# Turning the inverse of the delta rule over: VectorE in 32x32 blocks at levels 0 to 4, TensorE at level 5

## The reference

```python
k_beta = k * beta[..., None]
lower = jnp.where(strict, jnp.einsum('bhncd,bhnsd->bhncs', k_beta, k) * decay, 0.0)
rhs = jnp.concatenate([v * beta[..., None], k_beta * jnp.exp(g)[..., None]], axis=-1)
sol = lax.linalg.triangular_solve(lower, rhs, left_side=True, lower=True, unit_diagonal=True)
u, w = jnp.split(sol, 2, axis=-1)
```

## Time and profile before

| what | value |
|---|---|
| median of 3 runs | 4044.71 us (4038.54 to 4046.26) |
| the profiled execution | 4045.38 us, span 4043.6 us |
| mean granted TensorE clock | 0.976 |
| PE busy | 3901.0 us, 96% of the span |
| PEld busy | 3107.4 us, 77% |
| DVE busy | 2286.6 us, 57% |
| ACT busy | 1542.9 us, 38% |
| POOL busy | 491.4 us, 12% |

### The profile page before, as it was taken

The page is one execution under the profiler, slowest core; times in us unless marked ns, Lnnn a source line. Parts: engine busy times, 40 slices in busy tenths (PEclk is TensorE's granted clock), DMA queues, the critical chain, the costliest instruction groups (busy, mean ns, idle before and its releaser), DMA issues. The chain is left out here.

```text
span 4043.6 us, 47189 instructions
## 1 busy us (share of the span) xinstructions
PE 3901.0 (96%) x18086; PEld 3107.4 (77%) x18086; DVE 2286.6 (57%) x3149; ACT 1542.9 (38%) x2242; POOL 491.4 (12%) x366
## 2 busy tenths in 40 slices
PE   8999989999999998999989999999999999999997
PEld 6888668888788865888867678788877667878886
DVE  5445765445544565645567643675576663376656
ACT  3224643223322464322343534343343443443333
POOL 1001720000000163100020012200010002220002
PEclk9999989999999998999999989999999999999999
DMA  4333103333233320333331100122233100023222
GB/s 149 98 98 111 58 21 99 95 99 108 89 98 95 109 68 16 98 98 98 108 104 63 42 6 1 53 94 99 94 106 103 54 32 1 6 74 99 94 99 78
DMA packets 87022, 315.05 MB, mean 78 GB/s; under 512 B 10016, under 2 KB 10400, under 8 KB 86176
## 3 DMA queue, kind: packets, MB, share of 16 engines
q1 hardware_dynamic: 83664, 302.43, 23.5%
q10 hardware_dynamic: 3152, 9.74, 0.7%
HBM read 307.94 MB, written 2.10 MB: 77 GB/s over the span
## 5 line engine op out<-in xcount | busy, mean ns | idle before, releaser
L381 ACT ACTIVATE wh<-raw 128x1024 fp32r<-128x1024 f32 x564 | 597.4, 1059 | 1631.0 <-PE ps L401 1317.4
L399 PE MATMUL ps<-xh,wh 128*128 128x512 f32 x2336 | 918.0, 393 | 16.0 <-DVE xl L464 9.3
L400 PE MATMUL ps<-xl,wh 128*128 128x512 f32 x2336 | 910.8, 390 | 0.0
L401 PE MATMUL ps<-xh,wl 128*128 128x512 f32 x2336 | 910.7, 390 | 0.0
L385 DVE TENSOR_TENSOR wl<-raw,wh 128x1024 fp32r<-128x1024 f32 x564 | 694.2, 1231 | 190.9 <-ACT wh L381 190.1
L399 PEld LDWEIGHTS ps<-xh,wh 128*128 128x128 f32 x2336 | 439.8, 188 | 112.6 <-issue 19.8
L400 PEld LDWEIGHTS ps<-xl,wh 128*128 128x128 f32 x2336 | 439.9, 188 | 94.3 <-issue 3.6
L401 PEld LDWEIGHTS ps<-xh,wl 128*128 128x128 f32 x2336 | 439.7, 188 | 91.3
L399 PE MATMUL ps<-fh,wh 128*128 128x512 f32 x1016 | 397.4, 391 | 4.0 <-DVE wl L385 4.0
L400 PE MATMUL ps<-fl,wh 128*128 128x512 f32 x1016 | 395.4, 389 | 0.0
L401 PE MATMUL ps<-fh,wl 128*128 128x512 f32 x1016 | 395.4, 389 | 0.0
(11 more groups left out here) (465 smaller groups left out, 5656.6 us busy)
## 6 DMA issues: line engine op xcount, KB each, us to landing
raw<-in_w SPq DMA_DIRECT2D x564, 512.0 KB, 3.5
con<-in_consts SPq DMA_DIRECT2D x1, 2052.5 KB, 13.9
h<-in_x SPq DMA_DIRECT2D x4, 512.0 KB, 7.0
p_t<-in_p ACTq DMA_DIRECT2D x4, 512.0 KB, 4.3
w1k<-in_w1c ACTq DMA_DIRECT2D x2, 1024.0 KB, 4.9
w1v<-in_w1c ACTq DMA_DIRECT2D x2, 1024.0 KB, 7.2
out<-h SPq DMA_DIRECT2D x8, 256.0 KB, 2.1
dup_k<-roped ACTq DMA_DIRECT2D x8, 128.0 KB, 3.5
```

What stands on the lines that cost most here:

```text
L381: nc.scalar.activation(wh[k % 2][:, :], raw[k % 4][:, :], ACT.Copy).then_inc(s["w_hi"], 1)
L399: nc.tensor.matmul(DB[k % 2][:, :], a, hi(q), start=(q == order[0]), stop=False)
L400: nc.tensor.matmul(DB[k % 2][:, :], a, lo(q), start=False, stop=False)
L401: last = nc.tensor.matmul(DB[k % 2][:, :], b, hi(q), start=False, stop=(q == order[-1]))
```

## The change

At levels 1 to 4 the inverse is non-zero only within diagonal blocks of at most 32 tokens, so a transpose of each 32x32 block on its place is a transpose of the whole. Level 0 to 4 are now turned over by one VectorE instruction for each head, from `tri_t` straight to `tri` (both in SBUF), in the new function `dve_turn`. TensorE's transposes and ScalarE's copies of those levels are gone; level 5 keeps them, with a semaphore of its own (`tri_turned`). At levels 1 to 4 `dve_turn` stands right behind the subtraction of its head, inside `dve_upper`'s loop, and so ahead of the second head's subtraction and of all that follows in VectorE's queue. For level 0 of a later pair it stands ahead of the subtractions of level 6. In the first pair, the 14 idle matmuls keep their place in TensorE's queue. Pieces 10 and 11 of `pe_pre` are gone, and so are `act_tri0` and its place in ScalarE's queue.

```diff
--- before.py
+++ after.py
@@ -1568,7 +1568,8 @@
                     dve.wait_ge(s["tok_exp"], 1)
                     v.tensor_tensor(beg, bet, eg, ALU.mult).then_inc(s["kb_ready"], 1)
 
-                PIECES, READS = 12, 9
+                PIECES, READS = 10, 9
+                BLOCKS32 = 4
                 OFF = [0, 512, 896, 1152, 1280]
                 HEADS = (3, 4, 6, 7, 0, 1, 5, 2)
                 HSUM = {0: 0, 1: 2, 3: 4, 4: 6, 5: 8, 6: 10, 7: 12, 2: 14}
@@ -1599,9 +1600,12 @@
                 def pre_reader(t, i):
                     if i < READS:
                         return "pre_read", READS * t + i + 1
-                    if i == READS:
-                        return "eg_ready", t + 1
-                    return "tri_ready", PIECES * t + i - READS
+                    return "eg_ready", t + 1
+
+                def tri_count(t, lv, hd):
+                    if lv > BLOCKS32:
+                        return "tri_turned", 2 * t + hd + 1
+                    return "tri_ready", 2 * ((BLOCKS32 + 1) * t + lv) + hd + 1
 
                 def pe_pre(pe, s, t, i):
                     mm, tr = nc.tensor.matmul, nc.tensor.transpose
@@ -1626,13 +1630,8 @@
                     elif i < 9:
                         for b in range(NB):
                             ins = tr(bank[:, blk_of(b)], qkv[:, (3 if i == 7 else 6) + t, blk_of(b)], c("ident"))
-                    elif i == 9:
+                    else:
                         ins = mm(bank[:, :], c("pick2")[0:6, t * P:(t + 1) * P], g6, start=True, stop=True)
-                    else:
-                        hd = i - 10
-                        pe.wait_ge(s["tri0"], 2 * t + hd + 1)
-                        for b in range(NB):
-                            ins = tr(bank[:, blk_of(b)], tri_t[t % 2][hd][:, b, :], c("ident"))
                     ins.then_inc(s["pre_mm"], 1)
 
                 def dve_pre(dve, s, st, t, i):
@@ -1673,6 +1672,17 @@
                                                 c("ident").unsqueeze(1).to_broadcast([P, NB, P]), dec[hd][:, :, :],
                                                 ALU.subtract).then_inc(s["tri0"], 1)
 
+                def dve_turn(dve, s, t, lv, hd):
+                    if lv:
+                        dve.wait_ge(s["inv_ready"], turn(t, lv, hd) + 1)
+                    else:
+                        dve.wait_ge(s["tri0"], 2 * t + hd + 1)
+                        if t:
+                            dve.wait_ge(s["u_mm"], turn(t - 1, LEVELS, hd) + 1)
+                    nc.vector.transpose(tri[hd][:, :, :].rearrange("p b f -> p (b f)"),
+                                        tri_t[t % 2][hd][:, :, :].rearrange("p b f -> p (b f)"))\
+                        .then_inc(s["tri_ready"], 1)
+
                 def dve_qg(dve, s, st, t):
                     dve.wait_ge(s["eg_ready"], t + 1)
                     nc.vector.tensor_tensor(qkv[:, t, :], e_g[:, :], qkv[:, t, :], ALU.mult).then_inc(s["qg_ready"], 1)
@@ -1685,19 +1695,14 @@
                     act.wait_ge(s["pre_mm"], PIECES * t + 10)
                     nc.scalar.activation(e_g[:, :], pre_bank(t, 9)[:, :], ACT.Exp).then_inc(s["eg_ready"], 1)
 
-                def act_tri0(act, s, st, t):
-                    for hd in range(2):
-                        act.wait_ge(s["pre_mm"], PIECES * t + 11 + hd)
-                        nc.scalar.activation(tri[hd][:, :, :], view(pre_bank(t, 10 + hd)), ACT.Copy)\
-                            .then_inc(s["tri_ready"], 1)
-
                 def turn(t, lv, hd):
                     return (t * LEVELS + lv - 1) * 2 + hd
 
                 def pe_lower(pe, s, t, lv):
                     for hd in range(2):
                         pe.wait_ge(s["b_ready"], turn(t, lv, hd) + 1)
-                        pe.wait_ge(s["tri_ready"], PIECES * t + 2 * (lv - 1) + hd + 1)
+                        name, value = tri_count(t, lv - 1, hd)
+                        pe.wait_ge(s[name], value)
                         for b in range(NB):
                             ins = nc.tensor.matmul(DB[hd][:, blk_of(b)], low[hd][:, b, :], tri[hd][:, b, :], start=True,
                                                    stop=True)
@@ -1728,8 +1733,8 @@
 
                 def act_turned(act, s, st, t, lv):
                     for hd in range(2):
-                        act.wait_ge(s["tt_mm"], (t * (LEVELS - 1) + lv - 1) * 2 + hd + 1)
-                        nc.scalar.activation(tri[hd][:, :, :], view(DB[hd]), ACT.Copy).then_inc(s["tri_ready"], 1)
+                        act.wait_ge(s["tt_mm"], 2 * t + hd + 1)
+                        nc.scalar.activation(tri[hd][:, :, :], view(DB[hd]), ACT.Copy).then_inc(s["tri_turned"], 1)
 
                 def dve_upper(dve, s, st, t, lv):
                     for hd in range(2):
@@ -1737,6 +1742,8 @@
                         x = tri_t[t % 2][hd]
                         nc.vector.tensor_tensor(x[:, :, :], x[:, :, :], view(DB[hd]), ALU.subtract)\
                             .then_inc(s["inv_ready"], 1)
+                        if lv <= BLOCKS32:
+                            dve_turn(dve, s, t, lv, hd)
 
                 def pool_mask(pool, s, st, src, dst, level, name):
                     nc.gpsimd.tensor_tensor(dst[:, :, :], src[:, :, :],
@@ -2284,9 +2291,8 @@
                         pe_pre(pe, s, 0, i)
                     pe_sb(pe, s, 0)
                     for i in range(3, PIECES):
-                        if i == 10:
-                            pe_idle(DB[0], 0, 14)
                         pe_pre(pe, s, 0, i)
+                    pe_idle(DB[0], 0, 14)
                     pe_sb(pe, s, 1)
                     for t in range(GT):
                         for lv in range(1, LEVELS + 1):
@@ -2295,8 +2301,6 @@
                             pe_lower(pe, s, t, lv)
                             if slot < 15:
                                 pe_sb(pe, s, slot + 2)
-                            if lv == 6 and more:
-                                pe_pre(pe, s, t + 1, 10)
                             pe_upper(pe, s, t, lv)
                             if t and lv == 1:
                                 pe_out(pe, s, t - 1, 0)
@@ -2304,7 +2308,7 @@
                                 pe_new(pe, s, t - 1, lv - 1)
                             if more and lv <= 5:
                                 pe_pre(pe, s, t + 1, 2 * lv - 2)
-                            if lv < LEVELS:
+                            if BLOCKS32 < lv < LEVELS:
                                 pe_turned(pe, s, t, lv)
                             if t and 2 <= lv <= 4:
                                 pe_out(pe, s, t - 1, lv - 1)
@@ -2314,7 +2318,7 @@
                                 else:
                                     pe.wait_ge(s["eg_ready"], 1)
                                 pe_idle(BK[2], 0, 8)
-                            if more:
+                            if more and lv <= 5:
                                 pe_pre(pe, s, t + 1, 2 * lv - 1)
                         if not more:
                             pe_idle(BK[0], 0, 4)
@@ -2345,7 +2349,6 @@
                     act_sb(act, s, st, 0)
                     act_eg(act, s, st, 0)
                     act_sb_late(act, s, st, 0)
-                    act_tri0(act, s, st, 0)
                     act_sb(act, s, st, 1)
                     for t in range(GT):
                         for lv in range(1, LEVELS + 1):
@@ -2356,10 +2359,8 @@
                                 act_sb(act, s, st, slot + 2)
                             if lv == 2 and more:
                                 act_dec(act, s, st, t + 1, 0)
-                            if lv < LEVELS:
+                            if BLOCKS32 < lv < LEVELS:
                                 act_turned(act, s, st, t, lv)
-                            elif more:
-                                act_tri0(act, s, st, t + 1)
                             if lv == 2 and more:
                                 act_dec(act, s, st, t + 1, 1)
                             if lv == 5 and more:
@@ -2397,6 +2398,8 @@
                         dve_pre(dve, s, st, 0, i)
                     dve_qg(dve, s, st, 0)
                     dve_tri0(dve, s, st, 0)
+                    dve_turn(dve, s, 0, 0, 0)
+                    dve_turn(dve, s, 0, 0, 1)
                     dve_sb_late(dve, s, st, 1)
                     red = None
                     for t in range(GT):
@@ -2405,6 +2408,9 @@
                             more = t + 1 < GT
                             if slot < 15:
                                 dve_sb(dve, s, st, slot + 2)
+                            if more and lv == LEVELS:
+                                dve_turn(dve, s, t + 1, 0, 0)
+                                dve_turn(dve, s, t + 1, 0, 1)
                             dve_upper(dve, s, st, t, lv)
                             if t and lv == 1:
                                 dve_state(dve, s, st, t - 1, 0)
```

(2 more changed lines are left out.)

## The result

The changed kernel takes 4056.47 us in the median (4051.71 to 4060.57, 9 runs), the kernel before 4045.39 us (4038.54 to 4050.78, 9 runs): 11.1 us more, a ratio of 1.0027 with a 95% interval of 1.0018 to 1.0036. The time lies in the range of the prediction, but not where its likeliest case put it (4046.4, no change), and slower was given 0.28.

The account below looks back on a forecast made before the run. TensorE, busy 96%, was taken as the bound, its queue packed apart from one hole at the stage's start. -11.5 + 6.7 + 6.5 = +1.7 us on 4045.4 gives 4047.1, adjusted to 4046.4; range 4030 to 4066.

Parts of the forecast that it names:

- likeliest case: Whole kernel: the terms sum to about no measurable change, 4046.4 us; chance 0.35.
- slower: Sign of the whole change: a measurably longer time, chance 0.28, beside 0.57 for the same and 0.15 for faster.
- The start, -11.5 us: Start of the mixing stage, both layers: transposes and copies 1.44, waiting 2.74, clock 1.62 us in the first; -11.5 us together.
- VectorE's queue, +6.7 us: Levels of all pairs: instructions behind the new transposes start later and TensorE waits; 3.4 us a layer, +6.7 for both.
- The price D, 0.69 us: Length of one new VectorE transpose of 128x512 f32, taken as 0.69 us, between 0.42 and 1.23.
- the sum without falls: Start and queue with the clock holding in the levels: -4.8 us, 4040; as a rival, chance 0.17.
- The clock in the new gaps, +6.5 us: TensorE's longer idle gaps, eight levels a layer: four falls to half clock at 1.62 us each, +6.5 us.
- six as the most exposed: Gaps between 6-row matmuls, pair 0 levels 1 and 2, pair 1 level 1, two layers: likeliest places for clock falls.
- the start gives nothing: Rival at the stage's start: another wait replaces the logarithm's, leaving +13.2 us, 4058; chance 0.07.
- the clock falls in most gaps: Rival in the levels: half clock in all 16 gaps, +21 us, 4066; slower from eight falls on; chance 0.14.

Follow-up runs that it names:

- experiment 1: Kernel before, with only pair 0's level 0 turned over by VectorE and ScalarE's two copies ahead of the logarithm gone: 4032.51 us against 4046.26, ratio 0.9968.
- experiment 3: Changed kernel plus idle matmuls in all sixteen of TensorE's gaps in the levels: 4042.32 us, ratio 0.9993 to the kernel before.
- Experiment 2: Changed kernel with the second head's VectorE transpose at levels 1 to 4 moved behind dve_new, the state and the even piece's read: 4033.88 us, ratio 0.9973.
- experiments 1 and 7: Experiment 1 as above; the other: against the changed kernel, VectorE turns over level 0 alone, for all pairs; levels 1 to 5 on TensorE and ScalarE: 4029.74 us, 0.9965.
- Experiment 4: Changed kernel plus idle matmuls in six of the sixteen gaps (pair 0 levels 1 and 2, pair 1 level 1, both layers): 4049.81 us, ratio 1.0006.
- experiment 8: Changed kernel with the start undone: pair 0's level 0 on TensorE and ScalarE again, ahead of the logarithm: 4067.88 us against 4046.92, ratio 1.0058.

## Why the prediction came out as it did

- **The start, -11.5 us: right in size and in its wait, lucky in its clock.** ScalarE's copies held up the logarithm and TensorE waited for it; that wait is gone, and the first upper comes 6.0 us earlier (9.97 and 3.96 us). Alone the start measured -13.7, on top of the levels -11.4. But 1.62 us a layer of the forecast was the half clock at the first sums, and in the first layer of experiment 1 a fall of the same cost (10.70 - 9.05 = 1.65 us) stands in level 1 instead. The changed kernel has a fall in that place as well. In the profiled execution the total fits because the clock stood better elsewhere in the span, which the change is not shown to have caused; the wait alone, 8.4 us of the 11.5, is the part that is shown.
- **VectorE's queue, +6.7 us: right.** In the levels shown, the offsets up to the first instruction that waited agree to 0.04 us (3.77 for 3.73, 4.91 for 4.91, 4.08 for 4.07); the lower of pair 2 is 0.11 late (5.02 for 4.91). The first layer of experiment 3 has no fall in its levels and measures the queue: 167.90 us for 164.22, +3.7 a layer, where I had 3.4 (3.9 with D at 0.71):

```profile
2544.92 2.05 PE L1710 MATMUL ps<-tri_t,mid 128*128 128x128 f32 x16
```

```profile
2543.33 2.05 PE L1715 MATMUL ps<-tri_t,mid 128*128 128x128 f32 x16
```

  These are the last upper before (the first is at 2380.70) and in experiment 3 (the first is at 2375.43). The whole time of experiment 3 is 3.9 us under the kernel before (4042.32 against 4046.26; by the ratio's interval +0.8 to -6.5), where the sum without falls said -4.8, or -3.8 with D at 0.71. That is the sum of start and queue together, not the queue by itself. Experiment 2 shows that it is the order and not the work.
- **The price D, 0.69 us: right in kind.** It is 0.711, and the estimate worked out beside it from the Trainium skill ("VectorE: DVE Perf Modes", The three transpose paths) was 711 ns: by that rule, the trace agrees. Over 48 instructions the difference is 1.0 us.
- **The clock in the new gaps, +6.5 us: the step that failed, in its size.** "I take four falls" at 1.62 us each. The profile has six, and in each layer the one behind level 2 is twice as long; its rows are 0.91 + 1.73 us longer in the two groups shown above. In the profiled execution the six cost 11.5 us (5.8 a layer), 5 us more than I took. In the median of all executions the clock costs 14.2 us (experiment 3 against the changed kernel), 7.7 us more than I took, and that is most of the 10.1 us between forecast and median. The mean granted clock agrees: the median is 0.973 in the changed kernel and 0.977 in experiment 3, and a thousandth of the clock is 4 us of 4050.
- **What makes the clock fall.** I priced only the longer gaps. The runs show falls in the same places without a gap: at level 1 of pair 0 and of pair 1 in experiments 1 and 7 (lower takes 3.38 and 3.68 us, 3.41 and 3.68, in place of 2.05), behind a 6-row group, TensorE's transposes and another 6-row group, busy throughout. In the same places in experiment 3, with six and five idle matmuls over 128 rows between the two 6-row groups, the clock held. So neither the gap nor the transposes' removal is needed for a fall. What is shown is that dense matmuls in the gaps take the cost away; how much is due to the wait and how much to the thin work around it stays open, as no run filled the place with anything else.
- **Which gaps.** I named six as the most exposed, and in the profiled execution all falls stood there. Experiment 4 shows that this holds for that execution and not in general: with these six filled half of the cost stays, and the falls stand in other places. The falls differ from one execution to the next. The mean granted clock, which is recorded for every execution, is 0.974 in the profiled one of the changed kernel, the shortest (4051.71), and 0.972 or 0.973 in the other eight (4056.09 to 4060.57 us). In experiment 4 it goes from 0.977 (4041.91 us) to 0.973 (4056.07) with one and the same kernel. In which gaps the further falls stand only traces of those executions could show, and each kernel has one.
- **The rivals.** By time "the start gives nothing" came nearest (4058 for 4056.47), with a mechanism that experiment 1 rules out. By mechanism it is "the clock falls in most gaps" (+21 us with sixteen falls), and the truth lies between it and my case: 14.2 / 1.62 is about nine. It had 0.14. I drew its lower neighbour from one long wait (2.61 us) and one harmless stretch, and should have weighed that TensorE's work on both sides of most of the new gaps is over 6 or 64 rows. The kernel before shows a fall without any wait at the beginning of the same stage, where most of the work is over 6 or 64 rows: busy throughout, the clock goes from 1.00 to 0.50 (its windows):

```profile
2347.00:2349.00 2.00, 2.00 (x7) 0.48 (x4) 1.76 (x6) 0.00 (x1) 0.00 (x0) 1.00 0.00 0
2349.00:2351.00 2.00, 2.00 (x6) 0.80 (x5) 1.00 (x4) 1.60 (x3) 0.00 (x0) 0.60 0.00 0
2353.00:2364.00 11.00, 11.00 (x47) 9.62 (x48) 4.16 (x7) 0.49 (x1) 2.76 (x3) 0.50 0.01 2
```

## What to carry to other kernels

An engine busy for 57% of the span can still be the path: ask what stands behind a new instruction in its queue, and who waits for that. Moving one of two transposes behind the two things that TensorE waited for was worth 0.5%, without an instruction less. Work taken off TensorE was worth nothing here where its next input came from another engine. The clock can cost more than the queue (14.2 against 7.4 us), in places that differ from one execution to the next, and idle matmuls in the gaps took that cost away. One profile shows some of the exposed places, not the cost: compare the recorded clock and the times of all executions. Split a change by place: here two instructions a layer (the start) held most of the gain, and 24 a layer, at levels 1 to 4, the loss.

## What the runs showed of the hardware

- A VectorE transpose of 128x512 f32 in 32x32 blocks takes 0.711 us (668 to 714 ns over 60 instructions), about what a two-input operation of that shape takes (0.69), and 1.7 times a one-input one (0.42).
- The granted clock fell from 2.4 to 1.2 GHz after waits of TensorE of 0.8 to 1.9 us, mostly with matmuls over 6 or 64 rows around them, twice with 128 rows on both sides (experiment 4, 2535 and 3515 us). It also fell with no wait at all: behind 6-row groups and transposes (experiments 1 and 7), and at the start of the stage (2347 to 2351 us of the kernel before). Twelve f32 instructions of 128x128 (six idle matmuls, 1.6 us) in such a gap held it up in the profiled execution; six in a shorter gap (0.94 us) did not always.
- One fall can last for 20 us with TensorE busy throughout: in experiment 8 behind waits of 1.5 and 1.9 us (2398 to 2418 us), and at the start of the stage in the kernel before (2349 to 2369 us).
